# A recurrence kernel on one core: the state of two heads as one block-diagonal matrix, its output products on the whole PE array

## What is computed

```python
def step(S, inp):                       # S: heads x 64 (v) x 64 (k)
    r_t, w_t, k_t, v_t, kk_t, a_t = inp
    sa = jnp.einsum("bhvk,bhk->bhv", S, kk_t)
    S = (S * w_t[:, :, None, :]
         - sa[..., None] * (kk_t * a_t)[:, :, None, :]
         + v_t[..., None] * k_t[:, :, None, :])
    return S, jnp.einsum("bhvk,bhk->bhv", S, r_t)

oc_f, sc_f = scan_direction(con, 0, s0, False)
oc_b, sc_b = scan_direction(con, 1, s0, True)
ol_f, _ = scan_direction(lat, 0, sc_f, False)
ol_b, _ = scan_direction(lat, 1, sc_b, True)
```

## Time and profile before

| | us |
|---|---|
| three runs | 2496.74, 2504.0, 2504.55 |
| their median | 2504.0 |
| the profiled execution, its own time | 2506.32 |
| its span, first to last instruction | 2504.5 |
| chain steps, first to last product | 569 to 1180 |
| mean granted PE clock | 0.939 of 2.4 GHz |

### The profile page before, as it was taken

How to read it: one execution, slowest core, us unless ns; L and a number is a source line. 1 busy time by engine, 2 the same in 40 slices (tenths; PEclk the granted TensorE clock), 3 DMA queues, 4 the chain that set the end, 5 groups by cost and what they waited for, 6 DMA issues and landing times.

```text
span 2504.5 us, 59235 instructions
## 1 busy us (share of the span) xinstructions
PE 2127.5 (85%) x25824; PEld 1607.2 (64%) x25824; DVE 1303.3 (52%) x2180; ACT 1133.6 (45%) x1885; POOL 681.5 (27%) x412
## 2 busy tenths in 40 slices
PE   8799999267887888886879999997898898898878
PEld 2587777156766767775767666664666665666666
DVE  1357878523434444443346666663457652466752
ACT  2466767323433333443245545453355553355552
POOL 0335444210001111013233222223433432433332
PEclk9899999688998999998899999997999998899998
DMA  7215444553232322214222111112222211222222
GB/s 258 77 59 154 148 145 139 157 167 85 80 110 80 84 65 58 74 44 154 76 91 61 53 53 55 51 34 85 68 80 64 79 65 59 73 80 72 64 68 68
DMA packets 156162, 221.37 MB, mean 88 GB/s; under 512 B 84480, under 2 KB 109312, under 8 KB 155136
## 3 DMA queue, kind: packets, MB, share of 16 engines
q1 hardware_dynamic: 144800, 174.32, 22.5%
q0 software_dynamic: 9952, 40.11, 5.3%
q10 hardware_dynamic: 1152, 3.15, 0.3%
HBM read 164.85 MB, written 42.21 MB: 83 GB/s over the span
## 4 chain that ended last, share of the span: by engine, by line
PE 41%; DVE 10%; ACT 8%; issue 6%; POOL 2%; DMA 1%; DVEq 0%; ACTq 0%; POOLq 0%; SPq 0%
PE ps L259 6%; PE ps L261 6%; PE ps L260 6%; PE ps L2272 2%; PE ps L1379 2%; PE ps L2809 2%; PE ps L2232 1%; PE ps L2786 1%; PE ps L1369 1%; PE ps L1394 1%; ACT p L2292 1%; DVE pc L2875 1%; PE ps L398 1%; ACT wbh L239 1%; POOL wbl L244 1%
## 5 line engine op out<-in xcount | busy, mean ns | idle before, releaser
L244 POOL TENSOR_TENSOR wbl<-wb,wbh 128x1024 fp32r<-128x1024 f32 x128 | 308.7, 2412 | 655.6 <-ACT wbh L239 651.8
L259 PE MATMUL ps<-hTh,wah 128*128 128x512 f32 (+1 forms) x512 | 180.6, 353 | 17.2 <-POOL wal L244 10.7
L259 PE MATMUL ps<-hT2h,wbh 128*128 128x512 f32 x416 | 180.3, 433 | 10.8 <-POOL wbl L244 10.8
L260 PE MATMUL ps<-hTl,wah 128*128 128x512 f32 (+1 forms) x512 | 174.9, 342 | 0.0
L261 PE MATMUL ps<-hTh,wal 128*128 128x512 f32 (+1 forms) x512 | 174.8, 341 | 0.0
L259 PE MATMUL ps<-hT1h,wbh 128*128 128x512 f32 (+1 forms) x432 | 168.0, 389 | 3.1 <-POOL hT1l L2413 3.1
L239 ACT ACTIVATE wbh<-wb 128x1024 fp32r<-128x1024 f32 x128 | 134.6, 1052 | 68.7 <-PE ps L1951 43.4
L261 PE MATMUL ps<-hT2h,wbl 128*128 128x512 f32 x416 | 164.7, 396 | 0.0
L346 POOL TENSOR_TENSOR ro<-ro 128x256 f32<-128x256 f32 (+1 forms) x12 | 11.9, 995 | 561.0 <-DVE ro L330 561.0
L260 PE MATMUL ps<-hT2l,wbh 128*128 128x512 f32 x416 | 164.0, 394 | 0.0
L244 POOL TENSOR_TENSOR wal<-wa,wah 128x1024 fp32r<-128x1024 f32 x34 | 102.2, 3007 | 219.1 <-ACT wah L239 219.1
(11 more groups left out here) (411 smaller groups left out, 5524.8 us busy)
## 6 DMA issues: line engine op xcount, KB each, us to landing
wb<-in_w_in SPq DMA_DIRECT2D x56, 512.0 KB, 3.5
s_str_dram<-s POOLq DMA_DIRECT2D x48, 576.0 KB, 8.7
wm<-in_ada SPq DMA_DIRECT2D x48, 512.0 KB, 4.7
bkv<-s_str_dram SPq DMA_DIRECT2D x96, 192.0 KB, 3.1
wa<-in_rw_in SPq DMA_DIRECT2D x34, 512.0 KB, 4.1
wb<-in_da_in SPq DMA_DIRECT2D x32, 512.0 KB, 3.4
ARI<-s_str_dram SPq DMA_DIRECT2D x96, 128.0 KB, 3.3
wb<-in_w_out SPq DMA_DIRECT2D x16, 512.0 KB, 3.5
```

The lines of the kernel that those rows point to most:

```text
L244: e.tensor_tensor(self.lo[:, n % 2], self.raw[:, n % 3], self.hi[:, n % 2].bitcast(F32), ALU.subtract).then_inc(self.K.s.w_lo, 1)
L259: e.matmul(z, wh[:, k, :], hi[:, k, a:b], start=k == 0, stop=False)
L260: e.matmul(z, wh[:, k, :], lo[:, k, a:b], start=False, stop=False)
```

## The change

S grows from 64 to 128 columns for each (p, d). The first head of a pair keeps its 64x64 state in the upper left block and the second in the lower right one; the other two blocks are zero. The output products then take both heads at once: all 128 rows and 128 columns of weights, 64 columns streamed. The state products stay as they are, with the right block of S as what is streamed. VectorE writes each block on its own, so the scaling is two instructions of 64 partitions. The first memset clears all of S, both halves with the zero blocks. A gap in memory shrinks by what S grows, so nothing else moves.

```diff
-        self.gap = K.sb(c, "gap", [1024])
-        self.S = K.sb(c, "S", [2, 4, 64])
+        self.gap = K.sb(c, "gap", [512])
+        self.S = K.sb(c, "S", [2, 4, 128])
...
                     e.matmul(ps[half(j), 6 + p, blk64(2 * d + c)], G[half(j), p, blk64(2 * d + c)],
-                                 S[half(j), sc, 2 * p + d, :], start=False, stop=False, skip_group_check=True)
+                                 S[half(j), sc, 2 * p + d, blk64(j)], start=False, stop=False, skip_group_check=True)
             for d, p in QUADS:
                 c = h if d == 0 else 1 - h
-                for j in range(2):
-                    m = e.matmul(ps[half(j), 6 + p, self.place(u, d, c)], S[half(j), sc, 2 * p + d, :],
-                                 Q[half(j), p, blk64(2 * d + c)], start=False, stop=h == 1, skip_group_check=True)
+                m = e.matmul(ps[:, 6 + p, self.place(u, d, c)], S[:, sc, 2 * p + d, :], Q[:, p, blk64(2 * d + c)], start=False,
+                             stop=h == 1, skip_group_check=True)
             m.then_inc(s.ch_mm, 1)
...
-            pc = self.K.pcA[:, 2 * (u // 6):2 * (u // 6) + 2, a:b + 1:b - a]
-            e.tensor_tensor(S[:, 1 - sc].rearrange("x (p d) v -> x p d v", p=2),
-                            ps[:, 6:8, 0:256].rearrange("x p (q v) -> x p q v", v=64)[:, :, self.at_step(h), :],
-                            pc.unsqueeze(3).to_broadcast([128, 2, 2, 64]), ALU.mult).then_inc(s.ch_s, 1)
+            for j in range(2):
+                pc = self.K.pcA[half(j), 2 * (u // 6):2 * (u // 6) + 2, a:b + 1:b - a]
+                m = e.tensor_tensor(S[half(j), 1 - sc, :, blk64(j)].rearrange("x (p d) v -> x p d v", p=2),
+                                    ps[half(j), 6:8, 0:256].rearrange("x p (q v) -> x p q v", v=64)[:, :, self.at_step(h), :],
+                                    pc.unsqueeze(3).to_broadcast([64, 2, 2, 64]), ALU.mult)
+            m.then_inc(s.ch_s, 1)
...
-        e.memset(self.S[:, 0], 0.0).then_inc(s.s_set, 1)
+        e.memset(self.S[:, :, :, :], 0.0).then_inc(s.s_set, 1)
```

## The result

| | before | changed |
|---|---|---|
| median of 13 runs each, us | 2504.55 | 2523.24 |
| lowest and highest, us | 2491.61, 2512.03 | 2500.70, 2530.33 |
| the profiled execution, us | 2506.32 | 2509.10 |
| ratio, 95% interval | | 1.0059 (1.0038 to 1.0079) |

The change makes the kernel slower by 0.6%, 15 us. The ratio is taken over all runs of both and is not that of the two medians, which lie 18.7 us apart. The prediction had 23 us more, and a range of 2511 to 2542 that holds the median. A second series of the same kernel on another occasion gave 1.0048 (1.0023 to 1.0072), 12 us. The profiled execution of the changed kernel happens to be one of its fastest, 14 us under its median, so its span shows less of the change than the runs do.

A forecast was written before the change was run, and what follows sets the result against it. PE was taken to bound the recurrence. Products and switches at +34 us, less 10 given back in stalls and 1 for fewer rows, made +23 us: 2527 us against the median of 2504.0, range 2511 to 2542.

The forecast's parts named there:

- That PE bounds the stage, so that array time counts: Recurrence, 611 us: a microsecond more on PE is one more of time, except where it fills an "issue" stall.
- The whole-array row, 0.111 us: New output products: a row starts every 0.111 us, 8 rows take 0.89 us where eight old products took 0.465.
- The switches, 0.28 us: Each step's output products: going from quarter products to whole-array ones and back costs 0.28 us in all.
- What PE gets back, 10 us for the stalls and 1 us for the rows: PE in the recurrence: -10 us as "issue" stalls absorb added time, -1 us for 768 rows (three packets) fewer.
- an issue sum near 42: Sign in the profile after: PE's "issue" stalls over the recurrence sum to near 42 us rather than 53.
- a stage longer by 20: Sign in the profile after: the recurrence takes 611 us plus 20 or so.
- Stalls are PE waiting for instructions: PE's "issue" stalls, 53.1 us in 40, come from 16 KB fetch packets; about 3 packets in 10 end in one.
- VectorE at nothing: State's scaling: the second instruction, 15 to 20 us on VectorE, is covered and costs nothing; without cover +15.
- products at streaming speed: Rival, output products: weight loads hidden, a row every 0.058 us; 2506 us, no difference; chance 0.12.
- products priced by the row: Rival, output products: 8 rows cost 0.23 us, saving 0.23 us a step; 2492 us; chance 0.06.
- Nothing is given back: Rival, PE's stalls: they merely move behind the new products; +34 us, or +49 with VectorE; 2538 to 2553; chance 0.20.

The follow-up runs named there:

- experiment 3: Changed kernel with each whole-array output product done twice in a row: 1.0207 of before, 52 us over before and 37 over the change.
- 4: Kernel before with each quarter-array output product done twice: 1.0093 of before, 23 us slower.
- 6: Block-diagonal state, two scalings, old quarter-array output products, plus four zero-weight quarter-array products of 256 streamed columns per step: 1.0092 of before, 23 us slower.
- 5: Block-diagonal state, two scalings, old quarter-array output products, plus four zero-weight quarter-array products of 2 streamed columns per step: 1.0059 of before, 15 us slower.
- 9: Kernel before without the second head's output products, 768 rows fewer at the same array time: 1.0001 of before.
- 10: Kernel before without the second head's output and state products, 1536 rows fewer at the same array time: 0.9954 of before, 11.5 us faster.
- 1: VectorE's part alone: block-diagonal state, two scalings, larger memsets, with the quarter-array output products of before: 0.9996 of before.
- 2: Changed kernel with the scaling of the lower half of the partitions left out, one scaling per step, PE untouched: 1.0074 of before.

## Why the prediction was right, and where its sizes were off

**That PE bounds the stage, so that array time counts:** right, by experiments 3, 4 and 6, with a share of it that doesn't arrive.

**The whole-array row, 0.111 us:** right: doubling the products cost 0.89 us for 8 rows. The rule that was set against it, 60 cycles from start to start for a short product (the Trainium skill, TensorE: Matmul & The Clock Gate, "Back-to-back issue gap"), stands there for a product taken by itself. The same section says that in a stream of weight loads and products the spacing is set by both, and the 0.111 us of this trace agrees with that.

**The switches, 0.28 us:** nearly right in size. The step grew by 0.72 and 0.80 us where +0.70 was forecast, 36 us against the 34 of the sum. With 0.89 for the rows in place of 0.465, that leaves 0.30 us for the switches in a first step and 0.38 in a second.

**What PE gets back, 10 us for the stalls and 1 us for the rows:** this is the step that was mis-sized, and it is why the sum of 23 came out above the 15 measured. In the profiled executions the issue sum fell by 23 us (19 to 27 over the four profiles with the new products once each: 30.0, 34.1, 31.6 and 26.5 for 53.1), not by 11, and 36 less the 12 to 15 measured asks for 21 to 24. The prediction had named an issue sum near 42 and a stage longer by 20; neither came. Two terms were too small. The share of array time that disappears in stalls was taken as 3 in 10, from 40 stalls in 135 packets, as if an added microsecond met a stall by chance. Experiments 5 and 6 give 15 of 30 us by the issue sums. And a packet less was priced at the mean stall per packet, 0.4 us, where experiments 9 and 10 ask for some 1.3 or more. Put together, 36 us less half, less some 4 for three packets, is 14 us, within the 12 to 15 measured. That sum is fitted to the same runs and no test of its own. It also doesn't hold for large additions: of experiment 3's 43 us only some 6 disappeared, and its issue sum is 27.2 us where the change had 30.0. In every profile with the new products 26 to 34 us of stalls are left, and what experiment 3 added took next to nothing from them; why these remain is open.

**Stalls are PE waiting for instructions:** argued in the prediction from the packet size and the spacing, and not shown by any view. The experiments fit it: fewer rows with the same array time is faster (10, while 9 with half as many rows taken away showed no difference), more array time with the same rows shrinks the issue sum (6), more rows with little array time raises it (53.1 to 59.7, in 5). What sets the time of a fetch was not tried. The rule that fetches are mostly hidden (the Trainium skill, Runtime: NRT & Kernel Launch, "Instruction fetch mechanics") would have given the full 36 us, if these stalls are fetches; the 53.1 us of stalls before and the measured 15 us speak against it here.

**VectorE at nothing:** right (1 and 2), though its second half costs 0.57 us in a second step and not 0.32 to 0.42. The cover was idle time, and it was large enough.

**The rivals:** products at streaming speed and products priced by the row are excluded by the 0.111 us of the timeline and by experiment 3. "Nothing is given back" is excluded by the result itself, at most 20 us by its interval. The median lies within the stated range, but the upper end of 2542 stands in no sum: with nothing given back the sum is 2538 on the median and 2540 on the profiled execution.

## What to carry to other kernels

Count array time by starts, not instructions: four fp32 products on the whole array with weights of their own cost twice what eight quarter-array ones do that run two at a time, and a group of them between quarter-array work pays two switches more. Zero blocks in a stationary matrix are paid in full, as weight load. Where a dense stream of small products shows "issue" stalls, as here, added array time is partly paid out of these stalls, and taking rows away can gain time though no step gets shorter. And set the granted clock beside each time before two executions are compared: here single executions of one kernel differ by twice what the change costs, in step with their clock.

## What was not expected of the hardware

- Rows that run beside others are not free: leaving out 1536 product and weight-load rows that shortened no step made the kernel 11.5 us faster (0.9954, 0.9937 to 0.9970).
- Two instructions on VectorE, each on 64 partitions with 256 elements, took 0.89 us to the start of the next, where one on 128 partitions took 0.32 ahead of the output add and 0.50 ahead of a masked copy: neither the second nor its follower overlapped the one before as the output add had. Why is open.
- The same program's executions spread from 2500.7 to 2530.3 us, twice the change itself, and they do so in step with the clock granted to PE. Over the 13 runs of the result the fastest three had 0.942 to 0.946 of 2.4 GHz, and the slowest five 0.934 to 0.936. A profiled execution at 2501.7 us has its chain steps from 567.2 to 1171.0 us at a clock of 0.96, one at 2509.1 (the result's) from 570.2 to 1186.0 at 0.94. Why the clock differs between executions of one program was not tried.
